# The large products of a two-branch backbone layer: native f32 matmuls in place of three bf16 passes

## What is computed

```python
hn   = rmsnorm(x, norm1) * (1 + sc1) + sh1
proj = hn @ w_in                 # q, k, v, z, decays, u, gate_a, gate_b
o    = delta_net(q, k, v, decays)           # both directions, chunks of 64
y_a  = (rmsnorm(o, dn_norm) * silu(z)) @ w_br_a
y_s  = gelu(s5(u) + d * u)                  # both directions
y_b  = (y_s * sigmoid(y_s @ w_glu + b_glu)) @ w_br_b
x    = x + gt1 * ((sigmoid(gate_a) * y_a + sigmoid(gate_b) * y_b) @ w_out)
hn   = rmsnorm(x, norm2) * (1 + sc2) + sh2
x    = x + gt2 * ((silu(hn @ w_gate) * (hn @ w_up)) @ w_down)
```

## Time and profile before

| | |
|---|---|
| time, median of 3 runs | 4626.4 us (4625.68 to 4630.03) |
| span of the profiled execution | 4630.4 us |
| what the profile gives beside the span | nothing; the nearest of the three runs is 4630.03 us |
| busy: PE, PEld, DVE, ACT, POOL | 80%, 53%, 44%, 23%, 19% |
| PE's granted clock, mean | 0.89 of 2.4 GHz |

### The profile page before, as it was taken

One profiled execution on the slowest core, in us unless ns is written; L12 is line 12 of the kernel. 1 busy time (PEld: TensorE's weight loads), 2 busy tenths in 40 slices (PEclk: granted clock), 3 DMA queues, 4 the chain that ended last, 5 costly groups with the idle time before them and its releaser, 6 DMA issues. The chain is left out here.

```text
span 4630.4 us, 60884 instructions
## 1 busy us (share of the span) xinstructions
PE 3719.1 (80%) x22132; PEld 2456.7 (53%) x22398; DVE 2039.8 (44%) x3322; ACT 1080.3 (23%) x1702; POOL 890.1 (19%) x1040
## 2 busy tenths in 40 slices
PE   6568788888888797976854544599999699999997
PEld 2237575756666666755444444355454355555554
DVE  1236565656556565655459999422311211111112
ACT  0323232333232323232210011133211321111112
POOL 0010000000000000000067788011111011111110
PEclk8789898898989898989876777799999899999998
DMA  6210000000000000000311111221112011111111
GB/s 244 71 33 1 11 17 11 17 11 17 11 17 10 19 10 19 10 18 8 96 40 25 24 27 26 94 86 59 41 36 85 20 41 37 41 41 39 38 35 56
DMA packets 224662, 178.59 MB, mean 39 GB/s; under 512 B 24005, under 2 KB 211478, under 8 KB 222166
## 3 DMA queue, kind: packets, MB, share of 16 engines
q1 hardware_dynamic: 218214, 153.89, 11.4%
q10 hardware_dynamic: 4608, 11.54, 0.6%
q0 software_dynamic: 1648, 10.54, 0.6%
HBM read 144.39 MB, written 27.33 MB: 37 GB/s over the span
## 5 line engine op out<-in xcount | busy, mean ns | idle before, releaser
L171 POOL TENSOR_TENSOR w_pair<-w_raw,w_pair 128x1024 bf16<-128x1024 f32 (+1 forms) x156 | 345.9, 2220 | 2542.1 <-ACT w_pair L166 2542.1
L182 PE MATMUL m_out<-hn,w_pair 128*128 128x512 bf16 (+1 forms) x3102 | 569.3, 343 | 36.3 <-PEq L152 32.9
L182 PE MATMUL bank<-hn,w_pair 128*128 128x512 bf16 (+1 forms) x2220 | 480.3, 361 | 93.7 <-ACTq L1086 71.5
L182 PEld LDWEIGHTS m_out<-hn,w_pair 128*128 128x128 bf16 x3168 | 310.3, 98 | 294.9 <-issue 34.5
L182 PEld LDWEIGHTS bank<-hn,w_pair 128*128 128x128 bf16 x2304 | 225.8, 102 | 296.9 <-issue 131.3
L182 PE MATMUL m_out<-ys,w_pair 128*128 128x512 bf16 (+1 forms) x1552 | 288.6, 346 | 16.9 <-DVE ys L1996 15.0
L166 ACT ACTIVATE w_pair<-w_raw 128x1024 bf16<-128x1024 f32 x156 | 163.0, 1050 | 413.5 <-PE m_out L182 254.2
L1992 DVE TENSOR_TENSOR m_a<-m_out,m_sg 128x1280 f32<-128x1280 f32 x22 | 32.8, 1492 | 483.7 <-PE m_out L182 483.7
L1688 PE MATMUL s_banks<-u_block,m_block 128*128 128x160 f32 x128 | 40.9, 412 | 250.2 <-DVEq L1794 250.2
L182 PEld LDWEIGHTS m_out<-ys,w_pair 128*128 128x128 bf16 x1584 | 156.0, 99 | 149.6 <-issue 21.3
L182 PE MATMUL b_out<-ys,w_pair 128*128 128x512 bf16 (+1 forms) x1132 | 210.5, 345 | 5.2 <-PEq L1242 4.0
(11 more groups left out here) (346 smaller groups left out, 6460.6 us busy)
## 6 DMA issues: line engine op xcount, KB each, us to landing
w_raw<-in_w_in SPq DMA_DIRECT2D x56, 512.0 KB, 3.9
w_ada_rows<-in_w_ada SPq DMA_DIRECT2D x16, 1536.0 KB, 6.6
w_raw<-in_w_gu SPq DMA_DIRECT2D x44, 512.0 KB, 3.9
w_raw<-in_w_down SPq DMA_DIRECT2D x16, 512.0 KB, 4.0
scratch_x<-x_t POOLq DMA_DIRECT2D x1, 5120.0 KB, 16.4
scratch_o<-o_pair ACTq DMA_DIRECT2D x8, 640.0 KB, 3.9
scratch_u<-u_rows ACTq DMA_DIRECT2D x8, 640.0 KB, 2.9
u_block<-scratch_u SPq DMA_DIRECT2D x128, 40.0 KB, 1.8
```

What stands on the lines that cost most here:

```text
L171: pool.tensor_tensor(K.w_pair[:, slot, 1, 0:kt, :], K.w_raw[:, slot, 0:kt, :], K.w_pair[:, slot, 0, 0:kt, :], ALU.subtract).then_inc(K.w_l ...
L182: mm = pe.matmul(out[:, c0:c0 + cn], K.w_pair[:, slot, w, k, :], x[:, a, k, c0:c0 + cn], start=i < 3, stop=i >= 9 * kt - 3)
```

## The change

Weights and activations stay f32 and go into PE as they are. `w_raw` and `w_pair` become one tensor `w_tile` with two slots; the high and low halves, their copies and subtractions, POOL's part in the products and the semaphores between them are gone. A tile is 24 matmuls instead of 72. A load now waits until the product before in its slot is done. Results that were split are written in f32 by the instruction that makes them: the norm's scaling writes `hn`, gelu writes `ys`, the products of glu and MLP write `ys2` and `acts`, and a head's last DVE operation writes over `zs`, which is stored. The diff, cut to its core:

```diff
-    K.hn = sb("hn", [P, 2, KT, T], BF16)
-    K.w_raw = sb("w_raw", [P, 2, KT, P])
-    K.w_pair = sb("w_pair", [P, 2, 2, KT, P], BF16)
+    K.hn = sb("hn", [P, KT, T])
+    K.w_tile = sb("w_tile", [P, 2, KT, P])
...
 def load_tile(K, sync, q, slot, src, kt=KT):
-    sync.wait_ge(K.w_low, 2 * q + slot + 1)
+    sync.wait_ge(K.tile_done, 2 * q + slot + 1)
     sync.sem_inc(K.pulse, 1)
-    sync.dma_start(K.w_raw[:, slot, 0:kt, :], ...
+    sync.dma_start(K.w_tile[:, slot, 0:kt, :], ...
...
 def multiply_part(K, pe, slot, out, x, first, n, kt=KT):
     for i in range(first, first + n):
-        k, (w, a), (c0, cn) = i // 9, PASSES[i // 3 % 3], CHUNKS[i % 3]
-        mm = pe.matmul(out[:, c0:c0 + cn], K.w_pair[:, slot, w, k, :], x[:, a, k, c0:c0 + cn],
-                       start=i < 3, stop=i >= 9 * kt - 3)
+        k, (c0, cn) = i // 3, CHUNKS[i % 3]
+        mm = pe.matmul(out[:, c0:c0 + cn], K.w_tile[:, slot, k, :], x[:, k, c0:c0 + cn],
+                       start=i < 3, stop=i >= 3 * kt - 3)
...
 def multiply_tile(K, pe, q, slot, out, x, kt=KT):
-    pe.wait_ge(K.w_low, 2 * q + slot + 3)
+    pe.wait_ge(K.w_loaded[slot], (q + 1) * 16)
...
                 for a, n, c in SEGS:
-                    i = act.activation(t[:, k % 2, a:a + n], t[:, k % 2, a:a + n], ACT.Identity,
+                    i = act.activation(K.hn[:, k, a:a + n], t[:, k % 2, a:a + n], ACT.Identity,
                                        scale=mul[:, k, c:c + 1], bias=K.mod[:, shift * KT + k, c:c + 1])
                 i.then_inc(s_h, 1)
-                act.wait_ge(s_h, k + 1)
-                act.activation(K.hn[:, 0, k, :], t[:, k % 2, :], ACT.Copy).then_inc(s_hi, 1)
...
-                                first = 9 * KT * point // points
-                                tile_part(h + 1, t, first, 9 * KT * (point + 1) // points - first)
+                                first = 3 * KT * point // points
+                                tile_part(h + 1, t, first, 3 * KT * (point + 1) // points - first)
...
-                    third = 3 * KT
+                    third = KT
...
                     wait_tile(K, act, q0 + 2 * h + 1, 1)
+                    act.wait_ge(s.o_store, 16 * h + 16)
                     act.activation(zs[:, :], gemm_out[:, 0:T], ACT.Silu).then_inc(K.tile_read[1], 1)
-                    high_part(h + 1, 0)
-                    high_part(h + 1, 1)
...
                     act.wait_ge(s.o_fin, h + 1)
-                    act.wait_ge(s.o_store, 16 * h + 16)
-                    act.activation(opair[:, 0, :], os_[:, 0, 0:T], ACT.Copy).then_inc(s.o_high, 1)
-                    act.wait_ge(s.o_low, h + 1)
-                    act.wait_ge(s.o_high, h + 1)
-                    act.dma_start(K.scratch_o[bass.ds(h, 1)].rearrange("o p a t -> (o p) a t"), opair[:, :, :]).then_inc(s.o_store, 16)
+                    act.dma_start(K.scratch_o[bass.ds(h, 1)].rearrange("o p t -> (o p) t"), zs[:, :]).then_inc(s.o_store, 16)
...
-                pe.wait_ge(s_lo, KT + 1)
+                pe.wait_ge(s_y, KT + 2)
                 with pe.Fori(0, KT) as j:
                     multiply_tile(K, pe, q1 + j, 0, out[0], K.hn)
                     multiply_tile(K, pe, q1 + j, 1, out[1], ys2)
...
-                    pe.wait_ge(s_lo, f0 + n)
+                    pe.wait_ge(s_a, f0 + n + 1)
...
-                        dve.tensor_tensor(a[:, :], out[1][:, 0:T], sg[:, :], ALU.mult).then_inc(s_a, 1)
+                        dve.tensor_tensor(one(acts[i % 2], j), out[1][:, 0:T], sg[:, :], ALU.mult).then_inc(s_a, 1)
```

More of the change, by code:

```diff
@@ L501, in phase_decays @@
         pa = K.ps("pa", [P, 1536], st)
-        s_in, s_par, s_z, s_wh, s_wl = (K.sem("ba_" + n) for n in ("in", "par", "zeroed", "high", "low"))
+        s_in, s_par, s_z, s_wp = (K.sem("ba_" + n) for n in ("in", "par", "zeroed", "placed"))
         s_mm, s_act, s_dve, s_tr, s_pool = (K.sem("ba_" + n) for n in ("products", "act", "dve", "turned", "dup"))
@@ L523, in _ @@
                 pool.memset(par[:, :], 0.0).then_inc(s_z, 1)
[L524 to L530, removed]
+                pool.memset(wp[:, :, :, :], 0.0).then_inc(s_z, 1)
             @block.tensor
             def _(pe):
-                pe.wait_ge(s_wl, 1)
+                pe.wait_ge(s_wp, 4)
                 for j, out in ((0, pb), (1, pa)):
                     for k in range(KT):
[L537 to L540, removed]
+                        for c0, cn in CHUNKS:
+                            mm = pe.matmul(out[0:64, c0:c0 + cn], wp[:, j, k, :], K.hn[:, k, c0:c0 + cn],
+                                           start=k == 0, stop=k == KT - 1)
                     mm.then_inc(s_mm, 1)
@@ L561, in _ @@
                     for d, r in rows:
[L562 removed]
+                        act.activation(wp[:, j, :, r:r + H], w[:, :, 2 * H * j + H * d:2 * H * j + H * (d + 1)], ACT.Copy).then_inc(s_wp, 1)
                 act.wait_ge(s_mm, 1)
@@ L1240, in phase_branch_a @@
         s_sg, s_mg = K.sem("a_gate"), K.sem("a_mg")
-        s_in, s_v, s_g, s_hi, s_lo = (K.sem("glu_" + n) for n in ("in", "sum", "gelu", "high", "low"))
+        s_in, s_v, s_g = (K.sem("glu_" + n) for n in ("in", "sum", "gelu"))
         with K.nc.Block() as block:
@@ L1829, in phase_branch_b @@
         sg = K.sb("b_sg", [P, 2, T], stack=st)
-        y = K.sb("b_y", [P, 2, T], stack=st)
-        s_sg, s_y, s_hi, s_lo, s_t, s_mg = (K.sem("b_" + n) for n in ("sig", "y", "high", "low", "prod", "mg"))
+        y = K.sb("b_y", [P, T], stack=st)
+        s_y, s_t, s_mg = (K.sem("b_" + n) for n in ("y", "prod", "mg"))
         with K.nc.Block() as block:
@@ L1923, in _ @@
                         multiply_tile(K, pe, q0 + j, slot, out[slot], merged)
-            @block.scalar
-            def _(act):
-                with act.Fori(0, KT // 2) as j:
-                    for slot in range(2):
-                        split_high(K, act, q0 + j + 1, slot)
             @block.vector
@@ L1951, in phase_mlp @@
         sg = K.sb("m_sg", [P, T], stack=st)
-        a = K.sb("m_a", [P, T], stack=st)
-        s_a, s_hi, s_lo, s_x = (K.sem("m_" + n) for n in ("act", "high", "low", "x"))
+        s_a = K.sem("m_act")
         with K.nc.Block() as block:
@@ L1975, in _ @@
                         act.activation(sg[:, :], out[0][:, 0:T], ACT.Silu).then_inc(K.tile_read[0], 1)
-                        split_high(K, act, q + 1, 0)
-                        act.wait_ge(s_a, f0 + j + 2)
-                        act.activation(one(acts[i % 2][:, 0, :, :], j), a[:, :], ACT.Copy).then_inc(s_hi, 1)
-                        split_high(K, act, q + 1, 1)
-                    with act.Fori(0, KT // 2 - int(i == len(parts) - 1)) as j:
-                        for slot in range(2):
-                            split_high(K, act, loops[2 * i + 1][1] + j + 1, slot)
             @block.vector
```

140 lines of the change are left out of this document (26 added, 114 removed).

## The result

The changed kernel takes 5179.8 us, the kernel before 4628.2 (medians of four runs each): a ratio of 1.1192, with a 95% interval of 1.1176 to 1.1208. The profiled execution has a span of 5178.4 us, 548.0 over the 4630.4 of before.

The account below looks back on a forecast made before the run. The prediction took the products to be bound by PE's columns, the split costing time only where PE stands still for it. Its terms summed to +554.1: 4626.4 + 554 = 5180 us, range 5122 to 5230.

Parts of the forecast that it names:

- The price of a tile: All products: a tile of 8 k steps by 1280 columns goes from 12.98 to 17.18 us, 4.20 more.
- The rival of half-price columns: All products: f32 columns at half the price, a tile 8.59 us, the kernel about 3933 us; chance 0.02.
- Tiles in the scan: Three tiles inside the scan of each of seven heads: 11.7 us more a head, +81.9 in all.
- the one with more cover: Heads: fourth tile wholly hidden and half of the tap steps' columns too, 5136 us; chance 0.14.
- the variant with 0.1 us more a piece: Scans: each f32 piece of a tile costs 0.1 us more, +22; together with no gain of clock, chance 0.12.
- The fourth tile: In thirds at a head's start: two thirds bare, the last hidden, 2.46 us a head, +17.2 for seven.
- The heads' ends: High copy and low subtraction, for which all engines wait, go: 2.8 us less for each of eight heads, -22.4.
- The norms: Two norms: of 25.85 us, eight ACT pairs totalling 13.9 us are left, -11.9 each, -23.8.
- Waits between products: PE's waits shrink: MLP -8.4, before branch_b -4.3, before out -2.8; with -5.1 of clock, together -20.6.
- The gain of clock: MLP: with waits down to 2 us PE's clock stays up instead of 3.40 us at 0.50, -5.1 (bound 0).
- the variant that ended at 5207: Edges of the pieces in the scans (+22) and no gain of clock in the MLP (+5), 5207 us; chance 0.12.
- The wait before out: PE's wait of 9.6 us before the stage out: shorter by 2.8 us for the copy and subtraction that go.

Follow-up runs that it names:

- Four bf16 passes: The kernel before with a fourth bf16 pass, low weight by low activation, in every product, the split kept: 5264.7 us, ratio 1.1377 to before.
- the split put back: The changed f32 kernel with the copy to bf16 and the subtraction restored at each head's end, their halves unused: 5196.4 us.
- the kernel with 128 columns: The changed f32 kernel with the tiles' columns cut into ten of 128 in place of 512, 512 and 256: 5279.7 us in one run.
- four kernels: The changed f32 kernel and three variants of it: the split put back, 128 columns, and the last quarter of k steps left out (4528.1 us).
- the waits gone: The changed f32 kernel with PE's waits moved behind the first gate tile and ahead of a down tile's last k step: 5161.6 us.
- both parts: The kernel before with each head's split and store moved to the next head's start, and the waits of branch_b and MLP moved: 4558.6 us, 0.9853.
- the heads' part alone: The kernel before with only each head's split and store moved into the next head's start, other waits unchanged: 4588.0 us, 0.9917 of before.

## Why the prediction was right, point by point

- **The price of a tile** carries the result, and it came out to 0.01 us: 17.19 against 17.18. Four bf16 passes at 17.31 show what it is made of. The Trainium skill, FP8 and Floating Point Precision, section TensorE Precision Notes, gives true f32 four passes through the array; 17.19 / 4.33 = 3.97 agrees. The rival of half-price columns falls with it, and with it the reading of the Trainium skill (Perfetto Trace Analysis, section Engine Utilization) that stood beside it: a tile would have taken 8.6 us.
- **Tiles in the scan.** Forecast 11.7 a head, measured 12.27 in head 1 and 11.96 on the average of heads 1 to 6. That the columns stand bare between the hand-overs was right; of the variants the one with more cover is refuted, and of the variant with 0.1 us more a piece under a fifth is seen (0.57 us in head 1, 0.26 on that average, where 31 such pieces in seven heads would make 3.1 a head).
- **The fourth tile.** Forecast 2.46 a head, measured 2.41, but not as the text put it: the first third runs partly at half clock and alone costs 2.3 more (8.83 us up to the next product instead of 6.54), where 1.40 was reckoned; the second costs 0.75 more, and the sums behind it give 0.63 of that back. Only the last third behaved as the text has it: from its start to the next product it is 8.72 us before and after. The right number was in part luck.
- **The heads' ends.** Forecast -2.8, measured -2.92; the split put back gave 2.8 of wait and 2.1 net.
- **The norms.** Forecast -11.9 each, measured -13.0 in the wait ahead of the MLP and -13.4 in the first norm's stage. The 13.9 us that were to remain are 13.23: the scalings ran back to back.
- **Waits between products.** In the MLP -8.8 (15.0 to 6.2), forecast -8.4; before branch_b -4.6, forecast -4.3. The gain of clock, -5.1, is the step that failed: I expected full clock behind waits of 2 us, and it fell behind two of three, so that about a third of the gain came (an estimate: one of three stretches of 3.4 us at half clock is gone, 1.7 us). This is the no-gain half of the variant that ended at 5207, in the main come true. The slow beginning of the MLP also grew, from 2.6 to 5.7 us, at half clock 1.5 us lost. These 3.4 and 1.5 and the tiles' 0.7 (66 x 4.21) make most of the 6.0 that the MLP is over its forecast.
- **The wait before out** is mis-sized the other way, -5.0 for -2.8. The timeline of the kernel before shows what I had not counted:

```profile
3521.40 1.27 ACT L1865 ACTIVATE ys<-merged  x1 [14.26 <-DVE merged L1893]
3522.57 1.04 ACT L166 ACTIVATE w_pair<-w_raw 128x1024 bf16<-128x1024 f32 x1
3522.83 1.49 DVE L1895 TENSOR_TENSOR ys<-merged,ys  x1 [1.58 <-ACT ys L1865]
3523.69 2.61 POOL L171 TENSOR_TENSOR w_pair<-w_raw,w_pair 128x1024 bf16<-128x1024 f32 x1 [14.35 <-ACT w_pair L166]
```

The split of the next stage's weights was queued on ACT behind the copy of the result, and POOL was done only at 3526.30, 2.0 us after DVE's subtraction; the barrier waits for both. "The other copies and subtractions go from beside a busy PE: nothing" holds except at such a barrier.

- **out and the second norm** came out 3.8 low, which no term held: behind the shorter wait the tiles themselves grew by 32.3 us instead of 33.6 (106.97 to 139.27; over the first 6.8 us the clock is 0.77 where it was 0.55), PE's wait ahead of the sum of squares fell from 4.9 to 3.6, and the norm gave 1.1 more than forecast.
- **branch_a** came out 5.5 low: among the waits of before were 2.4 us for the loads of the heads' results, which are gone (a first tile of 17.2 us covers them), and 3.4 us at a clock of 0.50 behind it (2994.3 to 2997.7), half of them lost; and PE's wait at the stage's end fell from 4.0 to 2.7. I had given these waits no row.
- **Weights.** One buffer per slot costs nothing, as forecast: no wait on a load after the first tile.

The stages missed by between -5.5 and +6.0 us, and these nearly cancel, to -6.1 over the profiled executions. That the forecast of 5180 lies within 1 us of the median is due in part to that, and in part to the base: it was added to 4626.4, the median of three runs, where the median of four is 4628.2. The range is what the argument supported; its upper end, by the prediction's own terms (5207 and some 15), is 5222 and not 5230.

## What to carry to other kernels

On a PE-bound stretch, count column passes: native f32 is four, a bf16 split is three plus whatever of the splitting stands in front of PE, here 70 to 85 us of 4626. Read that second part from hand-overs and barriers, not from the busy times of the splitting engines, of which 588 us went on ACT and POOL alone and only those 70 to 85 were seen in the span. If the split is what hurts, move it off the hand-over (behind the next stage's first products, or ahead of the last k step) before giving up the cheaper passes: that gained 1.5% here, where f32 cost 12%.

## What the runs showed of the hardware that I had not expected

- f32 weight loads overlap one another: at 128 columns each shows 192 ns, and one is done every 112 (the kernel with 128 columns).
- After a wait of only 2.1 us PE's clock went to half for some 3.4 us, twice out of three times in the f32 kernel and in 8 of 12 over four kernels; with the waits gone there was no slow stretch in 1131 us.
- A shorter hand-over between heads (6.6 us of idle PE instead of 10.2) came with a gain above its length: where 3.6 us were taken out, the average of six heads fell from 235.6 us to 229.2 with both parts and to 229.9 with the heads' part alone. Of the 2 to 3 us beyond, 1.4 to 2.0 lie at the head's start, with earlier squares and, in some heads, a higher clock; the rest is not explained.
